# A mixture-of-experts block on one core: in the routed blocks GpSimd splits the down weights ahead of the scatter instead of behind it

## What is computed

```
out = zeros((n_tok + 1, d))
for each block of 128 rows (tok, w, e):        # rows sorted by expert, padded to 128
    y = (silu(x[tok] @ we_gate[e]) * (x[tok] @ we_up[e])) @ we_down[e] * w[:, None]
    out[tok] += y
```

## Time and profile before

| | us |
|---|---|
| median of 3 runs | 2814.5 |
| the runs | 2805.59, 2814.5, 2821.21 |
| the profiled execution, its own time | 2798.67 |
| its span, first to last instruction | 2797.0 |
| TensorE busy | 2543.7 (91%) |
| DVE busy | 1552.1 (55%) |
| GpSimd busy | 1384.4 (49%) |
| ScalarE busy | 1153.4 (41%) |

### The profile page before, as it was taken

The page is one execution under the profiler, slowest core; times in us unless marked ns, Lnnn a source line. Parts: engine busy times, 40 slices in busy tenths (PEclk is TensorE's granted clock), DMA queues, the critical chain, the costliest instruction groups (busy, mean ns, idle before and its releaser), DMA issues.

```text
span 2797.0 us, 49346 instructions
## 1 busy us (share of the span) xinstructions
PE 2543.7 (91%) x11232; PEld 1855.5 (66%) x11233; DVE 1552.1 (55%) x2764; ACT 1153.4 (41%) x1546; POOL 1384.4 (49%) x1726
## 2 busy tenths in 40 slices
PE   4999999957899998899999999999999999999990
PEld 1754664513456666688787877777887878777770
DVE  6379957993676776334333433444445544454535
ACT  5132313324233222344444444445555555555532
POOL 2011206013566665355555555565676677767662
PEclk7999999988899999999999999999999999999995
DMA  8152605454322322877777777788888988888978
GB/s 276 64 98 91 215 6 84 166 200 148 135 98 94 103 91 100 256 194 182 211 194 207 195 197 200 208 229 257 260 259 257 292 266 263 258 264 254 269 213 291
DMA packets 304953, 534.61 MB, mean 191 GB/s; under 512 B 38597, under 2 KB 204485, under 8 KB 304120
## 3 DMA queue, kind: packets, MB, share of 16 engines
q1 hardware_dynamic: 250248, 352.77, 38.0%
q0 software_dynamic: 51472, 173.70, 25.9%
q10 hardware_dynamic: 3168, 7.34, 0.7%
HBM read 395.75 MB, written 138.00 MB: 191 GB/s over the span
## 4 chain that ended last, share of the span: by engine, by line
PE 39%; issue 16%; POOL 8%; POOLq 6%; DVE 2%; DMA 1%; ACT 0%; SPq 0%; another core or an unknown queue 0%; ACTq 0%; DVEq 0%
PE psm L1122 29%; PE psm L1068 5%; PE psm L1115 3%; POOL arena L2265 2%; POOL arena L2262 2%; POOL st L2255 2%; POOLq L2261 1%; POOLq L2283 1%; POOLq L2274 1%; POOLq L2282 1%; POOL arena L2275 1%; PE psm L1090 1%; PE psm L1144 1%; POOL acc_d L2279 1%; DVE arena L2108 1%
## 5 line engine op out<-in xcount | busy, mean ns | idle before, releaser
L1122 PE MATMUL psm<-whi,xhi 128*128 (+1 forms) x1424 | 575.6, 404 | 42.5 <-issue 31.6
L1122 PE MATMUL psm<-whi,xlo 128*128 (+1 forms) x1424 | 559.4, 393 | 0.0
L1122 PE MATMUL psm<-wlo,xhi 128*128 (+1 forms) x1424 | 558.5, 392 | 0.0
L2009 DVE TENSOR_TENSOR arena<-psm,arena 128x256 f32<-128x256 f32 x178 | 75.5, 424 | 618.0 <-ACT arena L1504 612.7
L1122 PEld LDWEIGHTS psm<-whi,xhi 128*128 128x128 f32 x1424 | 269.5, 189 | 115.6 <-issue 65.0
L2270 POOL TENSOR_TENSOR wlo<-raw,whi (+1 forms) x64 | 331.0, 5172 | 20.3 <-ACT whi L1536 20.3
L1504 ACT ACTIVATE arena<-psm 128x256 f32<-128x256 f32 x178 | 68.2, 383 | 588.4 <-PE psm L1122 588.4
L1122 PE MATMUL psm<-whi,hhi 128*128 (+1 forms) x712 | 295.9, 416 | 14.3 <-POOL wlo L2270 7.0
L1122 PEld LDWEIGHTS psm<-whi,xlo 128*128 128x128 f32 x1424 | 269.2, 189 | 57.6
L2279 POOL DMA_INDIRECT acc_d<-arena x162 | 276.8, 1709 | 57.7 <-issue 53.7
L1122 PEld LDWEIGHTS psm<-wlo,xhi 128*128 128x128 f32 x1424 | 269.8, 189 | 50.9
(11 more groups left out here) (379 smaller groups left out, 4016.4 us busy)
## 6 DMA issues: line engine op xcount, KB each, us to landing
raw<-in_we_gate_dram SPq DMA_DIRECT2D x64, 1024.0 KB
raw<-in_we_up_dram SPq DMA_DIRECT2D x64, 1024.0 KB
raw<-in_we_down_dram SPq DMA_DIRECT2D x64, 1024.0 KB
arena<-in_w_ada_dram SPq DMA_DIRECT2D x12, 2048.0 KB
arena<-in_x_dram SPq DMA_DIRECT2D x32, 512.0 KB, 5.4
h_d<-arena SPq DMA_DIRECT2D x17, 512.0 KB, 2.7
arena<-in_w_in_dram SPq DMA_DIRECT2D x16, 512.0 KB, 6.2
mix_d<-bo SPq DMA_DIRECT2D x32, 256.0 KB, 2.3
```

Source lines behind the costliest of these rows:

```text
L1122: m = TE.matmul(o, a, w, start=(n == 0), stop=(n == len(todo) - 1))
```

## The change

In a step, the `If` with the split now stands ahead of `add_block`, behind the mark:

```diff
@@ -2285,9 +2285,9 @@
                 if not first:
                     pool.wait_ge(s_ya_out, (b - (NT + 1)) * 16)
                     PO.tensor_tensor(st[:, 59:60], mhalf[:, :], mhalf[:, :], ALU.add).then_inc(s_y_free, 1)
-                add_block(b - 1, 1 - w)
                 with pool.If(f > 0):
                     split_low((o & 1) * WSLOT, o + 1)
+                add_block(b - 1, 1 - w)
```

## The result

| | before | after |
|---|---|---|
| median of the runs, us | 2810.55 (4 runs) | 2990.08 (4 runs, 2983.14 to 2994.19) |
| ratio, 95% interval | 1 | 1.0647 (1.0613 to 1.0681) |
| span of the profiled execution, us | 2797.0 | 2991.3 |
| TensorE / GpSimd busy | 91% / 49% | 87% / 45% |

The forecast was 2960 us (+145 on the profiled execution), the range 2850 to 3070. The change costs 6.5%, in the way that was forecast; it is larger than forecast by a quarter (+180 between the medians, +194 between the two profiled spans).

What follows compares the result with a forecast made beforehand. GpSimd's loop of mark, scatter and landing, about as long as TensorE's step from the second stretch on, becomes the bound everywhere. Stretches +24.9, +97.8 and +22.3 make +145 on 2798.7, so 2944, plus 15.8 to the median: 2960 us, range 2850 to 3070.

Steps and rivals of the forecast that it cites:

- The signs that were named: Profile after: scatter 6 to 7 us behind the mark, split steps 14 to 15, L2287's wait over 450, TensorE near 85%.
- steps (3) and (4): Split step after the change: scatter starts 6.6 us after the mark, lands in 7.8; step 14.4 us (12.5 to 17.55).
- stretches: Routed blocks cut in three by how often GpSimd splits down weights, 71, 60 and 18 steps: +24.9, +97.8, +22.3 us.
- step (5): Steps without a split: plain ones 8.0 us, one per cycle that meets the gate and up loads 9.0 us.
- cycles of four: Second stretch: 15 cycles of two split steps, one plain and one loaded step, forecast at 45.8 us each.
- The bare landing: Rival, scatter's landing stays at the bare 6.4 us, split step 12.5: 2845 us, chance 0.08.
- The loads-ahead case: Rival, loads stand ahead of every split step's scatter, landing 10.35 us, step 17.55: 3151 us, chance 0.07.
- TensorE's clock: Rival, TensorE's clock falls in the new gaps, +62 us in the later stretches if none is absorbed: 3022 us, chance 0.11.
- The split waiting for ScalarE: Rival, GpSimd waits for ScalarE's late `whi` with the scatter queued behind, 1 us on 61 splits: 3020 us, chance 0.03.
- step (6): `wlo` ready some 2.2 us sooner for TensorE, which waited 7.0 us for it in all; costed at nothing.

Runs made afterwards that it cites:

- half split: Changed kernel with GpSimd's split in two instructions of 1024 columns, one ahead of the scatter, one behind it: 2907.9 us (1.0347).
- early indices: Row indices copied ahead of the wait for the last scatter: changed kernel 2967.0 us, kernel before 2813.9 us, changed kernel with light loads too 2804.0 us.
- partial loads: From the third expert on SP loads only one of eight parts of the weights: changed kernel 2868.7 us (1.0213), kernel before 2773.0 us (0.9867).
- the load held back: Changed kernel with SP's load of the next down weights released only behind the same step's scatter: 2951.9 us (1.0508).

## Why the prediction was right, and where its sizes were off

**The mechanism.** A landing of 6 us or more between scatter and next mark, covered by the split before and bare after, was the reason given, and the runs bear it out: without the split's length the loss is 38 instead of 180 us, and in the kernel before the split's absence turns into 187 us more of the mark's wait. The signs that were named came in kind: the split behind the mark (0.37 us), the mark's idle time of 3.7 to 4.2 us on the mean, the wait of L2287 at 533.6 us, the chain over GpSimd from the start, TensorE at 87%. Two sizes stand just outside of what was named: the scatter at 5.7 us after the mark (named 6 to 7), and split steps of 13.6 us (named 14 to 15).

**The split step, steps (3) and (4).** Forecast 14.4, measured 13.6 in the first two stretches. The time between mark and scatter was 0.9 too long: the split took 4.6 us there and not 5.2, since it doesn't run into the scatter's own work any more (in the earlier trace rows it begins 0.55 us before the scatter's instruction ends; in the half split the half ahead takes 2.39 us and the half behind, begun inside the scatter's instruction again, 2.97). The landing, 7.8, measured 7.84 and 7.89, but as the mean of two places: 7.46 us in the 26 split steps of the first two stretches whose down load was released 0.8 us ahead of the scatter, and 8.26 in the 26 where it was 0.4 us ahead. In the third stretch the step was 14.5 for other reasons: scatter at 8.2, landing 6.3. That is the collision with DVE, of which nothing stood in the forecast.

The Trainium skill's rule of taking turns (DMA: Bandwidth & Descriptors, Queues, rings and completion order) would have made the landing 8.2; the mean lies between it and mine, and the nearer loads' 8.26 comes close to the rule's. That an eighth of the load gives 6.2 to 6.3 and a whole one just ahead 7.5 to 8.3 agrees with it in kind.

**The steps without a split, step (5), were mis-sized.** I put the one that meets the gate and up loads at 9.0 and the others at 8.0. In cycles of four the first of the two takes 10.9 us (landing 9.0) and the second 8.1; in the third stretch the plain step takes 9.4. That is 9.07, 9.51 and 9.42 on the mean of the stretches against 8.22, 8.5 and 8.0, and 42 + 30 + 13 = 85 us over 49, 30 and 9 steps; the split steps gave 17 + 25 - 1 = 41 back. The net is the 43 us by which 145 missed 188. The reason behind the number was wrong as well: it held these steps' length before for TensorE's doing. The half split and the early indices show that landings beside loads bounded them already in the second stretch, and the trace of the kernel before had it to read: in the first of the two steps without a split of its 15 cycles the scatter takes 9.6 us on the mean to the next mark, which waits 3.5 of them idle. The forecast took 7.4 from a row of the third stretch instead.

**The sum.** First stretch +24.9 forecast, +49.4 measured; second +97.8 and +102.8; third +22.3 and +35.7. The second was right in its sum by two misses that cancel.

**The rivals.** The bare landing is what partial loads give (6.3) and not what full loads give. The loads-ahead case with its 10.35 us came in one split step, the last (10.8); the 61 in the three stretches landed in 7.6 on the mean. TensorE's clock did fall, to 0.98, 0.97 and 0.94 in the stretches, with gaps of up to 2.9 us, and its busy time grew by 59 us, 38 of them in the two later stretches, for which this rival put 62 (its 8 us of low clock behind each gap stand in no row). But the chain doesn't run over TensorE, so it had idle time to pay with, and with partial loads the second stretch lost 41 us at a clock of 1.00. The split waiting for ScalarE: 18.1 us in 2 waits, as before the change (20.3 in 2), so no.

**Gains costed at nothing, step (6).** Right: TensorE waited 10.0 us for `wlo` after, 7.0 before.

## What to carry to other kernels

Work that stands between issuing a transfer and waiting for it is free up to the transfer's landing time; moved in front of the issue, it lengthens the loop by up to its whole length, even if the engine's busy time doesn't grow. Here 61 splits of 4.6 us, some 281 us, cost 180, since the first stretch had a reserve of its own and the steps without a split got shorter in the first two. Before moving such work, look for the wait that it shortens: an idle time that is small in a step with the work and large in steps without it is a cover, not slack. And a landing is not a constant: beside loads an earlier issue ended no earlier here, so take its length from rows with the same loads around it, and expect an earlier issue to win less than it seems. If such rows show the wait bare already, there is no reserve there, whatever the busy shares say.

## What the runs showed of the hardware that was not expected

- **GpSimd and DVE hold each other up.** In the trace of the kernel after, DVE's split instructions (ns: min, median, max) have a longest of 5.6 us; before, the same view has 1.28 us as the longest:

```profile
L2025 DVE TENSOR_TENSOR wlo<-raw,whi x256: 1209/1217/5635, 1125.1 to 2863.6; - x124, 128x1024 fp32r<-128x1024 f32 x4
```

```profile
L2025 DVE TENSOR_TENSOR wlo<-raw,whi x256: 1209/1218/1279, 1123.2 to 2675.5; - x124, 128x1024 fp32r<-128x1024 f32 x4
```

  A DVE instruction of 1.2 us lasts up to 5.6 where GpSimd's split of 4.6 us runs beside it, and GpSimd's up to 5.6 too; with DVE's made thin GpSimd's are 4.63 at most. The Trainium skill (SBUF — State Buffer, SBUF: two separate sides) states that a DVE operation with two SBUF inputs and a GpSimd operation that reads SBUF lock each other out for a whole instruction; these rows agree.

- **A landing moves with its surroundings.** The same 128 x 1024 scatter with addition took 6.2 to 6.3 us from start to landing with an eighth of the loads. With a 1 MB load released 2.1 us behind its start (the load held back, second stretch) it took 6.2 on the mean where nothing else had been released, the bare time, and 7.4 where 2 MB had been released some 5 us ahead. With 1 MB 0.8 us ahead it took 7.5, 0.4 us ahead 8.3, 0.1 us ahead (early indices) 8.5, and 9.3 with 2 MB released 2.4 to 3.0 us ahead. Starting it 0.4 us earlier in the split steps of the second stretch made it 8.5 instead of 7.8.
